# PEER expert layer on one core: building the gate matrix in HBM by accumulating indirect transfers instead of one-hot matrix products

## What is computed

```python
q = (xt @ w_q).reshape(t, 8, 2, 128)                  # 8 heads, two halves
s1, s2 = q[:, :, 0] @ k1.T, q[:, :, 1] @ k2.T         # 128 keys each
v1, i1 = top_k(s1, 16); v2, i2 = top_k(s2, 16)
cand_s = v1[..., :, None] + v2[..., None, :]          # 16 x 16 sums
cand_i = i1[..., :, None] * 128 + i2[..., None, :]
top_s, pos = top_k(cand_s, 16)
idx = take_along_axis(cand_i, pos)                    # 16 experts of 16384 per head
g = softmax(top_s)
act = gelu(x . u_tab[idx])                            # u_tab, v_tab: 16384 x 1024
y = sum over heads and choices of (g * act) * v_tab[idx]
h = layer_norm(ALPHA * h + y)
```

## Time and profile before

| | |
|---|---|
| three runs | 1762.35, 1763.67, 1766.84 us, median 1763.67 |
| the profiled execution | 1766.34 us, of which its span (first to last instruction) 1764.5 us |
| busy shares of the span | TensorE products 95%, VectorE 75%, GpSimd 41%, ScalarE 37% |
| mean granted clock of TensorE | 0.985 |
| HBM | 349.4 MB read, 46.1 MB written |

### The profile page before, as it was taken

The page is one execution under the profiler, slowest core; times in us unless marked ns, Lnnn a source line. Parts: engine busy times, 40 slices in busy tenths (PEclk is TensorE's granted clock), DMA queues, the critical chain, the costliest instruction groups (busy, mean ns, idle before and its releaser), DMA issues. The chain is left out here.

```text
span 1764.5 us, 26964 instructions
## 1 busy us (share of the span) xinstructions
PE 1676.8 (95%) x8781; PEld 1456.0 (83%) x8781; DVE 1329.9 (75%) x2594; ACT 659.4 (37%) x1030; POOL 730.2 (41%) x668
## 2 busy tenths in 40 slices
PE   7998889699998999999999988999999999999997
PEld 5876644499998999899989987888888888888885
DVE  6679942378889889688789817778777777888866
ACT  3567740333334334233333323333333333333331
POOL 4744520284432111322145404445666666555401
PEclk9999999899999999999999999999999999999998
DMA  8422100333324467955988899999999989999972
GB/s 272 144 72 76 36 0 0 134 114 114 114 66 157 155 194 226 345 187 181 323 289 256 267 318 355 323 322 315 326 320 317 321 292 321 359 355 352 341 233 101
DMA packets 224427, 396.75 MB, mean 225 GB/s; under 512 B 15256, under 2 KB 154960, under 8 KB 224336
## 3 DMA queue, kind: packets, MB, share of 16 engines
q1 hardware_dynamic: 182800, 259.17, 43.8%
q0 software_dynamic: 36864, 134.23, 22.4%
q10 hardware_dynamic: 4672, 2.19, 0.4%
HBM read 349.40 MB, written 46.14 MB: 224 GB/s over the span
## 5 line engine op out<-in xcount | busy, mean ns | idle before, releaser
L722 PE MATMUL bank<-xhi,ut_hi 128*128 128x384 f32 x1024 | 356.2, 348 | 0.0
L722 PE MATMUL bank<-xhi,ut_lo 128*128 128x384 f32 x1024 | 345.3, 337 | 0.0
L722 PE MATMUL bank<-xlo,ut_hi 128*128 128x384 f32 x1024 | 345.2, 337 | 0.0
L814 POOL COPY row_index<-expert_rows 128x1 int32<-128x1 int32 (+1 forms) x256 | 158.0, 617 | 428.9 <-DVE gather_product L832 349.8
L1462 PE MATMUL bank<-v_hi,w_hi 128*128 128x512 f32 x768 | 240.9, 395 | 6.7 <-DVE w_lo L1583 6.7
L1462 PE MATMUL bank<-v_lo,w_hi 128*128 128x512 f32 x768 | 238.1, 391 | 0.0
L1462 PE MATMUL bank<-v_hi,w_lo 128*128 128x512 f32 x768 | 237.5, 390 | 0.0
L780 DVE TENSOR_TENSOR ut_lo<-bank,ut_hi 128x512 fp32r<-128x512 f32 x216 | 141.4, 684 | 118.3 <-ACT ut_hi L739 117.1
L819 POOL DMA_INDIRECT gathered<-in_peer_v,row_index x128 | 182.3, 1424 | 107.1 <-POOLq L818 101.4
L1499 ACT ACTIVATE v_hi<-v_raw 128x1024 fp32r<-128x1024 f32 x128 | 135.6, 1060 | 238.1 <-PE bank L1462 231.1
L1556 DVE TENSOR_TENSOR v_lo<-v_raw,v_hi 128x1024 fp32r<-128x1024 f32 x128 | 156.3, 1221 | 62.2 <-ACT v_hi L1499 62.2
(11 more groups left out here) (178 smaller groups left out, 2662.5 us busy)
## 6 DMA issues: line engine op xcount, KB each, us to landing
u_raw<-in_peer_u SPq DMA_DIRECT2D x128, 512.0 KB, 4.9
v_raw<-in_peer_v SPq DMA_DIRECT2D x128, 512.0 KB, 5.7
g_in<-gate_matrix SPq DMA_DIRECT2D x128, 192.0 KB, 4.2
activations<-gel SPq DMA_DIRECT2D x96, 192.0 KB, 2.9
a_in<-activations SPq DMA_DIRECT2D x96, 192.0 KB, 4.5
gate_matrix<-stage SPq DMA_DIRECT2D x15, 1152.0 KB, 7.7
w_in<-in_w_in SPq DMA_DIRECT2D x28, 512.0 KB, 3.8
wq<-in_peer_wq SPq DMA_DIRECT2D x16, 512.0 KB, 4.2
```

Of the source, the lines that this page charges most:

```text
L722: ins = self.nc.tensor.matmul(self.bank[b + (r % 2) * spare][:, 0:DTOK], u[r % 2][:, k, :], x[:, k, 0:DTOK], start=(i == 0), stop=(i == 3 ...
L814: nc.gpsimd.tensor_copy(self.index[r][:, :], self.rows[:, bass.ds(k, 1)]).then_inc(self.index_ready, 1)
```

## The change

The one-hot rows, their products, `stage` and its stores are dropped. The gate matrix is zeroed in HBM by 22 plain DMAs from a tile of zeros, issued by SyncE inside the mixer's loop, and each gate is then *added* at its place by an indirect DMA on GpSimd's queue: 128 single float32 elements (one per token of a block) per DMA, 8 heads x 3 token blocks x 16 choices = 384 DMAs. Selection is done per head for all four token blocks at once. Heads 0 to 2 are selected inside `queries`, the other five in the first 20 blocks of the new stage `activations`, which takes the place of `gates`. 60 of the 384 scatters are issued in `queries`, six per step from step 6 on, and 324 in `activations`, between the fetches. `MADE` goes from 96 to 112, so `activations` makes 93 blocks and `experts` 16. `U_FROM` goes from 80 to 96; live stretches use five fetched tiles per two steps, later steps one. The copy and wait ahead of each fetch go. The first loads of `experts` are issued at the end of `activations`. All loops are written out. The core of it:

```diff
-FIRST = 3
-EXTRA = (3, 7, 7)
-BESIDE_TOKENS = 16
-CLOSING = 9
-MADE = BY_QUERIES + FIRST + sum(EXTRA) + DT * BESIDE_TOKENS + CLOSING
+MADE = 112
 RING = 4
-U_FROM = sum(BESIDE) * GATE_TURNS + sum(BETWEEN)
+U_FROM = 96
+ZERO_ROWS = 6
+ZEROED = -(-KEYS // ZERO_ROWS)
+SCATTERS = QH * DT * TOPK
+PICKED = (1, 7, 11)
+WEIGHED = (3, 9, 13)
+SCATTER_FROM, SCATTERS_EACH = 6, 6
...
+class GateCells:
+    def zero(self, eng, n):
+        at = slice(n * ZERO_ROWS, min((n + 1) * ZERO_ROWS, KEYS))
+        eng.dma_start(self.matrix[at, :, :].rearrange("i j t -> j i t"),
+                      self.zeros[:, :].unsqueeze(1).broadcast_to([P, at.stop - at.start, DTOK])
+                      ).then_inc(self.zeroed, 16)
+    def scatter(self, eng, n):
+        q, tb, k = n // (DT * TOPK), n // TOPK % DT, n % TOPK
+        if n == 0:
+            eng.wait_ge(self.zeroed, 16 * ZEROED)
+        if n % (DT * TOPK) == 0:
+            eng.wait_ge(self.listed, q + 1)
+        if k == 0 and q > 0:
+            eng.wait_ge(self.landed[tb][(q - 1) % 2], 16 * TOPK * ((q - 1) // 2 + 1))
+        self.nc.gpsimd.indirect_dma_start(
+            out=self.flat, out_offset=bass.IndirectOffsetOnAxis(ap=self.at[:, tb, q, k:k + 1], axis=0),
+            in_=self.gate[:, tb, q, k:k + 1], in_offset=None, compute_op=ALU.add).then_inc(self.landed[tb][q % 2], 16)
...
+class Selection:
+    def places(self, eng, q, link):    # less maximum, two places, keys and places to bf16
+    def pick(self, eng, side, link):
+        V, shape = self.nc.vector, [P, TB * TOPK, TOPK]
+        flat = self.hit.rearrange("p b k j -> p (b k) j")
+        link(V.tensor_tensor(out=flat, in0=self.placef[:, side, :].unsqueeze(2).broadcast_to(shape),
+                             in1=self.iotab[:, :].unsqueeze(1).broadcast_to(shape), op=ALU.is_equal))
+        link(V.tensor_tensor(out=self.hit[:, :, :, :], in0=self.hit[:, :, :, :],
+                             in1=self.keyf[:, :, side, :].unsqueeze(2).broadcast_to([P, TB, TOPK, TOPK]),
+                             op=ALU.mult))
+        link(V.tensor_reduce(self.sel[:, side, :, :].rearrange("p b k -> p (b k)"), flat, AX.X, ALU.add))
+    def weigh(self, eng, q, link):     # rows of the sparse block, cells of the dense ones, softmax
...
 class GatherPath:
-    def start(self, eng, kind, q, j):
+    def start(self, eng, q):
+        kind, k, r = q // SLOTS, q % SLOTS, q % RING
+        if kind == 0 and k % TOPK == 0:
+            eng.wait_ge(self.cells.listed, k // TOPK + 1)
+        after(eng, self.used, q - RING + 1)
-        nc.gpsimd.tensor_copy(self.index[r][:, :], self.rows[:, bass.ds(k, 1)]).then_inc(self.index_ready, 1)
-        eng.wait_ge(self.index_ready, 2 * q + 1)
-        eng.sem_inc(self.index_ready, 1)
...
 # queries, GpSimd
+                    if n >= SCATTER_FROM:
+                        for i in range(SCATTERS_EACH):
+                            cells.scatter(eng, (n - SCATTER_FROM) * SCATTERS_EACH + i)
 # queries, VectorE
+                    if n in PICKED:
+                        picks.places(eng, PICKED.index(n), link)
+                        picks.pick(eng, 0, link)
+                        picks.pick(eng, 1, link)
+                    elif n in WEIGHED:
+                        picks.weigh(eng, WEIGHED.index(n), link)
-def gates(nc, sem, bank, ident, iota, acts, far, act_dram, top, pos, key, gates_dram):
+def activations(nc, acts, far, act_dram, cells, picks, feed):
...
+        @block.vector
+        def _(eng):
+            for m in range(BY_QUERIES, MADE):
+                s = m - BY_QUERIES
+                q, part = part_of(s)
+                if part == 0:
+                    picks.places(eng, q, link)
+                elif part == 1:
+                    picks.pick(eng, 0, link)
+                elif part == 2:
+                    picks.pick(eng, 1, link)
+                elif part == 3:
+                    picks.weigh(eng, q, link)
+                acts.lower_pair(eng, m + 1, m + 1)
+                for q in range(used_by(s), used_by(s + 1)):
+                    far.use(eng, q)
+        @block.gpsimd
+        def _(eng):
+            left = SCATTERS - scattered
+            for q in range(U_FROM):
+                far.start(eng, q)
+                if q >= RING - 1:
+                    each = lambda i: scattered + min(left, -(-left * i // (U_FROM - RING - 2)))
+                    for n in range(each(q - RING + 1), each(q - RING + 2)):
+                        cells.scatter(eng, n)
+            for q in range(U_FROM, U_FROM + RING):
+                far.start(eng, q)
+        @block.sync
+        def _(eng):
+            for m in range(BY_QUERIES, MADE):
+                acts.load_ahead(eng, m, m)
+                if m == MADE - 3:
+                    feed.load_first_rows(eng)
+                elif m == MADE - 2:
+                    cells.wait_for_all(eng)
+                    feed.load_first_weights(eng)
+                acts.store(eng, m, m, act_dram)
...
 # experts
+    used_by = lambda n: min(2 * SLOTS, U_FROM + 5 * min(n, TAIL) // 2 + max(n - TAIL, 0))
```

More of the change, by code:

```diff
@@ L105, in build @@
         pB = sb("pB", [P, PC_END])
-        mixer(nc, a, sem, bank, h, ident, ones, iota, small, pB)
+        cells = GateCells(nc, sem, sb, gates_dram)
+        mixer(nc, a, sem, bank, h, ident, ones, iota, small, pB, cells)
         xhi = sb("xhi", [P, KD, T], F32R)
@@ new lines, in experts @@
+def experts(nc, a, sem, bank, h, small, acts, far, act_dram, feed, out):
+    V, S, G = nc.vector, nc.scalar, nc.gpsimd
+    SLOT = feed.SLOT
+    TAIL = 2 * (KEYS - MADE)
+    STEPS = KEYS
+    CLOSE = STEPS - SLOT
+    LAST = (DT, *range(DT))
+    is_live, block_of = feed.is_live, feed.block_of
+    used_by = lambda n: min(2 * SLOTS, U_FROM + 5 * min(n, TAIL) // 2 + max(n - TAIL, 0))
+    WEIGH = min(n for n in range(STEPS) if used_by(n) >= SLOTS)
+    FAR_DONE = min(n for n in range(STEPS) if used_by(n) >= 2 * SLOTS)
+    assert used_by(WEIGH) == SLOTS and FAR_DONE + 6 <= CLOSE
@@ L1521, in step @@
+                    if n == STEPS - 2:
+                        v_upper(n + 1)
                     if more:
-                        acts.upper_half(eng, 1, m + 1, r + 1, 0)
-                v_upper(0, 0, 1)
-                v_upper(1, 1, 1)
-                steps(eng, step, between=lambda: far.gelu(eng))
+                        acts.upper_half(eng, 1, m + 1, m + 1, 0)
             @block.gpsimd
             def _(eng):
-                def start(tiles):
-                    for kind, q, j, _ in tiles:
-                        if not (isinstance(q, int) and q < U_FROM + RING):
-                            far.start(eng, kind, q, j)
@@ L1535, in step @@
-                def step(n, i, t, tiles):
-                    if t is None:
-                        ahead = q_of(n) + 2
-                        for q in range(q_of(n) if n == TAIL else ahead, min(ahead + 1, 2 * SLOTS)):
-                            far.start(eng, 1, q, q)
-                    elif not (isinstance(n, int) and n + 1 == TAIL):
-                        start(tiles(i + 1))
-                steps(eng, step)
-                eng.wait_ge(far.index_ready, 2 * 2 * SLOTS)
+                for q in range(U_FROM + RING, 2 * SLOTS):
+                    far.start(eng, q)
@@ L1629, in far_block @@
                         spread(DT)
-                v_lower(0, 0)
-                v_lower(1, 1)
-                steps(eng, step, between=lambda: far.weigh(eng))
+                v_lower(0)
+                for n in range(STEPS):
+                    step(n)
                 for tb in range(DT):
```

662 lines of the change are left out of this document (250 added, 412 removed).

## The result

The changed kernel takes 2037.14 us (2034.15 to 2041.98), the kernel before 1763.77 us beside it (1762.35 to 1766.84). The ratio is 1.155, with a 95% interval of 1.1521 to 1.1579: **15.5% slower**, where 1670 us had been forecast. The profiled execution took 2041.98 us, its span is 2040.2 us.

The account below looks back on a forecast made before the run. TensorE was taken as the bound, busy 1676.8 of 1764.5 us. 1650 us after savings, plus 2 mixer, 3 queries, 11 activations and 4 experts, made 1670 us; range 1645 to 1800.

Parts of the forecast that it names:

- 1.0 us per DMA back to back: GpSimd in `activations`: each scatter or fetch costs 1.0 us, the next being prepared while one runs.
- the term that decides: `activations`: GpSimd needs 424 x 1.0 + 56 = 480 us against TensorE's 469, so +11 us.
- My upper bound of 788 us for GpSimd: GpSimd's time in `activations` if each DMA took the late steps' mean of 1.858 us: +319 us.
- Collisions: `activations`: one DMA per block meets a two-input VectorE instruction of 1.22 us half way, 0.6 x 93 = 56 us.
- A full instruction lost per block, 113 us: `activations`, by the skill's port-lock rule alone: 1.22 us lost per block makes the term 68 us, time 1727 us.
- GpSimd becomes the bound: Rival, in `activations`: accumulating scatters may issue slower than fetches, 1.42 us each, giving 1782 us; chance 0.28.
- the 1.37 at which I let it decide: Scatter time in us at which GpSimd's cost in `activations` and `queries` eats the remaining gain of 107 us.
- Tiny transfers clog the queue: Rival, in `activations`: 324 scatters landing one after another at 5.2 us each, about 2880 us; chance 0.03.
- What goes: One-hot products -88 us, stalls in gates and at its change to experts -24, blocks moved from experts -4: 1650 us.
- The mixer: 22 zero stores on SyncE's queue between loads of `w_in`: 2 us, range 0 to 15.
- Queries: VectorE's selection for three heads leaves it about 3 us late at the stage's end: 3 us, 0 to 8.
- Experts: Five tiles per two live steps bring DMA to 345 GB/s, close under 356: 4 us, 0 to 22.

Follow-up runs that it names:

- e1_plain: The changed kernel with its 384 scatters writing instead of adding, so some gates are lost: 1813.54 us.
- e3_half: The changed kernel with only the first 8 of each head's 16 choices scattered, 192 DMAs instead of 384: 1709.32 us.
- e4_late: The changed kernel with all 384 scatters issued in `activations` and none in `queries`: 2095.41 us.
- e9_after_spread: The complete changed kernel with `U_FROM` 112 instead of 96 and four uses of fetched tiles per pair of live steps instead of five: 2039.07 us.
- e5_spread: The kernel of e2_none with `U_FROM` 112 instead of 96 and four uses of fetched tiles per pair of live steps instead of five: 1655.9 us.
- e2_none: The changed kernel with no scatters issued, the gate matrix left zero; zeroing, selection and fetches stay: 1694.46 us.
- e8_ring5: The kernel of e2_none with five tiles in the ring instead of four, a narrower tile of zeros and each zero store cut in three: 1670.06 us.
- the estimate in 4: A line through two median issue times: the changed kernel, and the same with each scatter cut to 64 of its 128 partitions, which took 1982.16 us.

## Why the prediction was wrong

**The step that failed** is "1.0 us per DMA back to back", in the term that decides. It has two errors, both of one sign. The issue of an accumulating scatter is 1.54 us, not 0.97: I took the fetch as nearest row for an operation that does one thing more (e1_plain: 0.58 us of it is the addition). The gap in front of a DMA does not vanish with the copy and the semaphore step; 0.30 us of the 0.81 stays, in front of the fetches too, which take 1.31 us for it. The first is 324 x 0.54 = 175 us, the second 424 x 0.30 = 127. With them, and collisions 13 us below mine, the term is 769 - 469 = +300 us, not +11; e3_half, e4_late and e9_after_spread show that GpSimd's sum decides, by costing 0, 111.6 and 22.3 us where the sum says 0, 118 and 21. My upper bound of 788 us for GpSimd was nearly the truth, for another reason: the late steps' 1.858 us held collisions.

Between forecast and measurement lie 367 us: 289 of them are this term, 62 `queries` and 20 `experts` (below), 371 in all.

**Collisions** were of the size that I had given them. If all that a scatter takes over 1.54 us is collisions, they are 324 x (1.673 - 1.54) = 43 us in `activations`, where I had said 56. The Trainium skill, SBUF — State Buffer, "Who interferes with whom", has the port pair locked for a whole instruction. Single rows agree: the scatter at 766.78 took 0.38 us longer, and VectorE's instruction with two inputs had run since 766.06 and ended 0.51 us after the scatter's start:

```profile
766.06 1.23 DVE L957 SCALAR_TENSOR_TENSOR gather_product<-gathered,h 128x1024 f32<-128x1024 f32 x1 [5.25 <-DMA gathered<-in_peer_u,expert_rows]
```

A full instruction lost per block, 113 us, did not come.

**The rival *GpSimd becomes the bound*** is what happened, at the place it named. Its price was too low, since it put a scatter at 1.42 us and left out the gap, and its threshold was too high: e1_plain stands at 1.34 us per scatter, under the 1.37 at which I let it decide, and is 47 us slower than before, because the fetches, `queries` and the ring in `experts` had taken the margin already. I gave the forecast 0.45 because 1.424 "comes from a stretch where VectorE hardly leaves the ports". That weighed the rows on collisions, of which I had some; on the addition I had none, and between ends that far apart the low one had no claim. *Tiny transfers clog the queue* fell: a scatter lands in 3.7 us at the median and the next are issued meanwhile.

**What goes** was right. e5_spread, where neither the scatters nor the ring cost anything, has a span 110.4 us shorter than before; I had 88 + 24 + 4, less 3 in `queries`, 113. The 4 was misread from two single instructions: a pair of live steps took 13.28 us, not 13.46, and 16 x (13.28 - 8.16 - 5.04) is 1 us. In e2_none the middle stretch is TensorE at 100% from 600 to 1020 us, as plain blocks. **The mixer** was charged 2 us, and no cost can be told from the scatter of the runs: `queries` begins (its first upper part of the query weights) at 332.1 us, before at 329.7, but at 329.4 to 332.2 in the other kernels with the same mixer. In 52 to 190 us TensorE is busy for 129.97 us, before 129.58, with the DMA share at 0.75 instead of 0.28:

```profile
52.00:190.00 138.00, 129.97 (x546) 99.94 (x545) 112.63 (x113) 94.55 (x117) 72.91 (x35) 0.98 0.75 253
```

**Queries**: 3 us forecast, 64.7 measured. VectorE's part is 7 to 16 us (the kernels without scatters there). In e2_none two of its nine waits for scores are left, 17.6 of 39.9 us, so the sum of what it does more was about right; but I had set it against the sum of its spare time, and from the third wait on it had none in hand when a longer step came. The scatters' part is 49 to 58 us (e4_late and the kernels without scatters). My own working, six scatters against 6.6 us of idle time in each of ten steps, gives 4.5 us a step at 1.85 us each. The wait of the first scatter was missing from it altogether, with what is queued behind it.

**Experts**: I said 4 us for five uses per pair, by bytes per second, with 22 as the end. It cost about 24 (e8_ring5, e9_after_spread). The term was right to worry but asked the wrong thing: not how many bytes cross, but how long one tile is away, 8.5 to 10.9 us where it held the chain, against four tiles and five uses. The upper end of the range, 1800, came from leaving out scatters above 1.47 us, and that is where the truth lay.

## What to carry to other kernels

Before work is moved to an engine that looks idle, multiply: the number of instructions there by issue time *and* the gap in front, against the time of the stage they must fit in; below it they cost nothing, even where the engine is full for 100 us, and above it all of the excess, since what that engine feeds is queued behind. An operation that no row shows is not priced by its nearest relative if it does one thing more; take as many of them as fit at the upper bound, here one token block of three. And a ring of buffers, as here, can be too short for its landing times while bytes per second are still free.

## What the runs showed of the hardware

An accumulating indirect DMA of 128 single elements held GpSimd for 1.54 us, a plain one 0.96, and 64 accumulating elements 1.41: most is paid per DMA (some 1.27 of 1.55 by the estimate in 4). In front of each stood 0.30 us in which nothing else was waited for, and which was there with the addition and without it. That is 115 us of GpSimd's time in the scatters alone.

VectorE can also be the one that waits. In e2_none its shift of 128x64 integers, 0.19 us at the median of eight, took 2.39 us once, from 511.18 on, beside a subtraction of GpSimd with two inputs that ran from 511.12:

```profile
511.18 2.39 DVE L209 TENSOR_SCALAR place<-pos 128x64 uint32<-128x64 uint32 x1
...
511.12 2.39 POOL L1123 TENSOR_TENSOR wq_lo<-wq,wq_hi 128x1024 fp32r<-128x1024 f32 x1
```

Small elements weigh on the DMA engines more than their bytes: between 700 and 800 us, with 38 scatters, e3_half shows them busy to 0.87 at 254 GB/s, e2_none, with the same blocks and no scatters, to 0.79 at 252.
